# Norm boundaries of a 159-slab transformer kernel: two slabs interleaved by chunk, a third pair of PSUM banks, and the sums of squares on VectorE

## What is computed

```python
for i in range(2):                       # first_block
    h = rms_norm(x, g[i][0])
    h = mlstm_mixer(h, ...) if i == 0 else short_conv_mixer(h, ...)
    x = x + rms_norm(h, g[i][1])         # "post" norm, then the residual
    h = relu(rms_norm(x, g[i][2]) @ w_up[i]) ** 2 @ w_down[i]
    x = x + rms_norm(h, g[i][3])         # "post" norm, then the residual
# second_block
h = rmsnorm(x, mix_norm_g)               # retention and pooling from one projection
x = x + concat([y_ret, y_pool]) @ w_out
x = x + cross_attn(rmsnorm(x, xa_norm_g), rmsnorm(mem, mem_norm_g), ...)
x = x + conv_glu_ffn(rmsnorm(x, ffn_norm_g), ...)
return rmsnorm(x, final_norm_g)
```

## Time and profile before

| | |
|---|---|
| median of 3 runs | 994.25 us (993.46 to 1000.04) |
| the profiled execution | 992.6 us |
| its span, first to last instruction | 990.5 us |
| TensorE busy | 961.8 us (97%) |
| VectorE busy | 648.3 us (65%) |
| ScalarE busy | 537.0 us (54%) |
| GpSimd busy | 144.2 us (15%) |

### The profile page before, as it was taken

One profiled execution on the slowest core, in us unless ns is written; L12 is line 12 of the kernel. 1 busy time (PEld: TensorE's weight loads), 2 busy tenths in 40 slices (PEclk: granted clock), 3 DMA queues, 4 the chain that ended last, 5 costly groups with the idle time before them and its releaser, 6 DMA issues.

```text
span 990.5 us, 20138 instructions
## 1 busy us (share of the span) xinstructions
PE 961.8 (97%) x8062; PEld 950.9 (96%) x8062; DVE 648.3 (65%) x839; ACT 537.0 (54%) x754; POOL 144.2 (15%) x129
## 2 busy tenths in 40 slices
PE   8999989999999899989999999899999999999996
PEld 8999989999999899989999999899999999999995
DVE  6567576665444877587655444894775779999642
ACT  5566656654443555556555444565554557666541
POOL 2121140000010400159000000414120110000001
PEclk9999999999999999999999999999999999999998
DMA  9533636555545355545455553663433545555521
GB/s 337 198 128 111 217 123 207 194 197 191 207 169 202 109 203 191 190 134 207 170 195 188 179 203 113 217 210 130 163 136 127 171 144 197 201 180 177 206 86 43
DMA packets 25844, 172.17 MB, mean 174 GB/s; under 512 B 3252, under 2 KB 3892, under 8 KB 5432
## 3 DMA queue, kind: packets, MB, share of 16 engines
q1 hardware_dynamic: 25784, 171.30, 49.7%
HBM read 170.24 MB, written 1.05 MB: 173 GB/s over the span
## 4 chain that ended last, share of the span: by engine, by line
PE 80%; DVE 7%; issue 1%; POOL 1%; ACT 1%; DVEq 0%; ACTq 0%; POOLq 0%
PE po L403 25%; PE po L404 24%; PE po L405 24%; DVE xnL L1241 3%; DVE wL L1234 2%; PE po L431 1%; PE po L432 1%; PE po L430 1%; POOL rtok L1810 1%; PE pc L732 1%; PE pn L471 1%; PE pn L481 1%; DVE y L1441 0%; PE pn L710 0%; PE pa L710 0%
## 5 line engine op out<-in xcount | busy, mean ns | idle before, releaser
L794 ACT ACTIVATE wH<-raw 128x1024 fp32r<-128x1024 f32 x318 | 335.4, 1059 | 297.9 <-PE po L405 267.5
L1234 DVE TENSOR_TENSOR wL<-raw,wH 128x1024 fp32r<-128x1024 f32 x318 | 387.8, 1244 | 157.0 <-ACT wH L794 156.6
L403 PE MATMUL po<-xnH,wH 128*128 128x256 f32 x1376 | 392.2, 285 | 15.2 <-DVE xnL L1241 12.4
L404 PE MATMUL po<-xnL,wH 128*128 128x256 f32 x1376 | 385.1, 280 | 0.0
L405 PE MATMUL po<-xnH,wL 128*128 128x256 f32 x1376 | 385.1, 280 | 0.0
L403 PEld LDWEIGHTS po<-xnH,wH 128*128 128x128 f32 x1376 | 262.3, 191 | 19.3 <-DVE xnL L1241 10.3
L404 PEld LDWEIGHTS po<-xnL,wH 128*128 128x128 f32 x1376 | 260.4, 189 | 0.2
L405 PEld LDWEIGHTS po<-xnH,wL 128*128 128x128 f32 x1376 | 260.0, 189 | 0.0
L403 PE MATMUL po<-hH,wH 128*128 128x256 f32 x688 | 192.0, 279 | 0.0
L404 PE MATMUL po<-hL,wH 128*128 128x256 f32 x688 | 192.0, 279 | 0.0
L405 PE MATMUL po<-hH,wL 128*128 128x256 f32 x688 | 192.0, 279 | 0.0
(11 more groups left out here) (283 smaller groups left out, 1052.7 us busy)
## 6 DMA issues: line engine op xcount, KB each, us to landing
raw<-in_weights SPq DMA_DIRECT2D x158, 1024.0 KB, 4.8
x<-in_xT SPq DMA_DIRECT2D x4, 256.0 KB, 6.4
raw<-in_weights SPq DMA_DIRECT2D x2, 512.0 KB, 6.3
mem<-in_memT SPq DMA_DIRECT2D x1, 1024.0 KB, 12.7
out<-y SPq DMA_DIRECT2D x4, 256.0 KB, 2.4
decayt<-in_decay SPq DMA_DIRECT2D x1, 512.0 KB, 3.7
poolwt<-in_poolw SPq DMA_DIRECT2D x1, 256.0 KB, 3.7
par<-in_params SPq DMA_DIRECT2D x1, 164.0 KB, 3.4
```

The costliest lines, as they stand in the source:

```text
L403: pe.matmul(psum[:, n, 0:T], wH[w][:, wc], aH[:, ac, :], start=start, stop=False)
L404: pe.matmul(psum[:, n, 0:T], wH[w][:, wc], aL[:, ac, :], start=False, stop=False)
L794: act.activation(wH[b % HL][:, hs], raw[b % RAW][:, hs], ACT.Copy).then_inc(s_hi, 1)
L1234: dve.tensor_tensor(wL[b % HL][:, hs], raw[b % RAW][:, hs], wH[b % HL][:, hs].bitcast(f32), ALU.subtract)\
```

## The change

At each of the four norm boundaries:

- TensorE runs the first two slabs of the next phase (`up0`, `cin`, `up1`, `rq`) together, chunk by chunk (`slab_pair`): chunk k of slab 0, then chunk k of slab 1. It waits for the input per chunk, no longer per pair of chunks.
- `pa` and `pb` become one pair of banks `third`. The key fillers `f0` to `f3` and the third slab (number 2) of each of those phases use it; slab 3 then waits for slab 1's drain. The other groups keep `po[g % 2]`.
- The sums for the new norm are taken in the third slab, after its chunk 0, and the spread after its chunk 3.
- The four adds of squares are on VectorE (four instructions, at the end of its `boundary`), and so are all adds of `y` to `x`; GpSimd keeps only the power there. The first pair of chunks is scaled and added as two single chunks.
- The weight splits, and in `boundary` of ScalarE and VectorE the order of all steps, are laid out anew; VectorE now splits one more half slab before the scaling at boundary 2.

At the two residual boundaries both halves of a split were one after the other; now the next input (`xnH`, `xnL`) of a pair stands between them, the first half ahead of it. The squares and their adds on GpSimd stay there.

```diff
-NORMS = ["pre", "pre", "post", "pre", "post", "pre", "post", "pre", "post", "pre", "pre", "pre", "last"]
+NORMS = ["pre", "pre", "post", "preV", "post", "preV", "post", "preV", "post", "preV", "pre", "pre", "last"]
...
-        pa = ctx.enter_context(nc.psum_tensor("pa", [P, 512], f32))
-        pb = ctx.enter_context(nc.psum_tensor("pb", [P, 512], f32))
+        third = ctx.enter_context(nc.psum_tensor("third", [P, 2, 512], f32))
+        pa, pb = third[:, 0, :], third[:, 1, :]
...
+        in_third = [GROUP0[name] for name in ("f0", "f1", "f2", "f3")]
+        in_third += [GROUP0[name] + 2 for name in ("up0", "cin", "up1", "rq")]
+
+        def place_of(g):
+            return 2 if g in in_third else g % 2
+
         def slot(g):
-            return po[g % 2]
+            return third if g in in_third else po[g % 2]
...
-                if g >= 2:
-                    e, n = DRAIN[g - 2]
+                before = [b for b in range(g) if place_of(b) == place_of(g)]
+                if before:
+                    e, n = DRAIN[before[-1]]
                     pe.wait_ge(s_drain[e], n)
...
+            def slab_pair(name, aH, aL, feed, between={}):
+
+                s, g = SLAB0[name], GROUP0[name]
+                for k in range(8):
+                    pe.wait_ge(s_xn, 8 * feed + k + 1)
+                    for j in range(2):
+                        if k == 0:
+                            slot_free(g + j)
+                        if k % 4 == 0:
+                            weights_ready(s + j, k // 4)
+                        for n in range(2):
+                            mm = products(slot(g + j), n, (s + j) % HL, k, aH, aL, k, k == 0, k == 7)
+                        if k == 3:
+                            mm.then_inc(s_half, 1)
+                        if k == 7:
+                            mm.then_inc(s_slab, 1)
+                    if k in between:
+                        between[k]()
...
+                if NORMS[n] == "preV":
+                    pe.wait_ge(s_sqv, squares_summed(n + 1))
+                else:
+                    pe.wait_ge(s_sqa, squares_added(n + 1))
...
-                for j in range(4):
-                    phase_slab(up, j, xnH, xnL, ready=(s_xn, 4 * feed) if j == 0 else None,
-                               between=norm(n_norm) if j == 1 else {})
+                slab_pair(up, xnH, xnL, feed)
+                for j in range(2, 4):
+                    phase_slab(up, j, xnH, xnL, between=norm(n_norm, 0, 3) if j == 2 else {})
...
-                        slab(i * 4 + (s0 + 4 + j), (s0 + j) % HL, slot(g0 + j), xnH, xnL)
+                        slab(i * 4 + (s0 + 4 + j), (s0 + j) % HL, slot(g0 + 4 + j), xnH, xnL)
...
-            for i in range(12):
-                phase_slab("cin", i, xnH, xnL, ready=(s_xn, 8) if i == 0 else None, between=norm(5) if i == 1 else {})
+            slab_pair("cin", xnH, xnL, 2)
+            for i in range(2, 12):
+                phase_slab("cin", i, xnH, xnL, between=norm(5, 0, 3) if i == 2 else {})
...
-            for i in range(4):
-                phase_slab("rq", i, xnH, xnL, ready=(s_xn, 16) if i == 0 else None, between=norm(9) if i == 1 else {})
+            slab_pair("rq", xnH, xnL, 4)
+            for i in range(2, 4):
+                phase_slab("rq", i, xnH, xnL, between=norm(9, 0, 3) if i == 2 else {})
...
+            def boundary(post, gain, up, value=None):
+
+                def feed_chunk(c):
+                    act.wait_ge(s_xadd, 5 * post + c + 1)
+                    act.activation(xnH[:, c, :], x[:, c, :], ACT.Identity, scale=col(gain, c)).then_inc(s_xnH, 1)
+
+                def feed(p):
+                    feed_hi(p, gain, (s_xadd, 5 * post + p + 2))
+
+                s = SLAB0[up]
                 if value is not None:
-
-                    split(nxt)
+                    split(s, halves=(0,))
+                    feed_chunk(0)
+                    feed_chunk(1)
+                    split(s, halves=(1,))
                     fill_values(value)
-                    nxt += 1
-                for p in range(4):
-
-                    feed_hi(p, gain, (s_xadd if p % 2 else s_xaddV, 2 * post + p // 2 + 1))
-                    if p < 2:
-                        feed_squares(p)
-                split(nxt, halves=(0,))
+                    feed(1)
+                    split(s + 1, halves=(0,))
+                    feed_squares(0)
+                    feed_squares(1)
+                else:
+                    split(s + 1, halves=(0,))
+                    feed_chunk(0)
+                    feed_chunk(1)
+                    feed_squares(0)
+                    split(s + 1, halves=(1,))
+                    feed(1)
+                    feed_squares(1)
+                if value is not None:
+                    split(s + 1, halves=(1,))
+                feed(2)
                 feed_squares(2)
+                feed(3)
                 feed_squares(3)
-                split(nxt, halves=(1,))
...
-                for n in range(4):
+                split(s0 + 2)
+                split(s0 + 3)
+                keep_R(n_norm, Rs[:, :])
+                square(0)
+                square(1)
+                for n in range(2, 4):
                     split(s0 + n + 2)
-                    if n == 0:
-                        keep_R(n_norm, Rs[:, :])
                     square(n)
...
-                split(SLAB0["out2"] + i + 2)
-                feed_pair(i, "gxa", residual("out2")(i))
+                split(SLAB0["out2"] + i + 2, halves=(0,))
+                feed_hi(i, "gxa", residual("out2")(i))
+                split(SLAB0["out2"] + i + 2, halves=(1,))
+                feed_squares(i)
...
-                k.then_inc(s_xn, 1)
+                    k.then_inc(s_xn, 1)
...
             def boundary(n, post, filler, feeds, gain, key):

-                nxt = SLAB0[filler] + 1
-                two = nxt == SLAB0[f"f{key}"]
-                split(nxt, halves=(0,))
+                first = SLAB0[filler] + 1
+                two = first == SLAB0[f"f{key}"]
+                split(first, halves=(0,))
                 mean_square(n)
-                split(nxt, halves=(1,))
-                if two:
-                    split(nxt + 1, halves=(0,))
-
+                split(first, halves=(1,))
+                split(first + 1, halves=(0,))
                 dve.wait_ge(s_R, n + 1)
...
-                    dve.tensor_tensor(xs, xs, ys, ALU.add).then_inc(s_xaddV, 1)
-
-                scale(0)
-                add(0)
+                    dve.tensor_tensor(xs, xs, ys, ALU.add).then_inc(s_xadd, 1)
+
+                link(dve.tensor_tensor(y[:, 0, :], y[:, 0, :], pn[:, 128:128 + T], ALU.mult))
+                dve.tensor_tensor(x[:, 0, :], x[:, 0, :], y[:, 0, :], ALU.add).then_inc(s_xadd, 1)
+                dve.tensor_tensor(y[:, 1, :], y[:, 1, :], pn[:, 128:128 + T], ALU.mult).then_inc(s_t, 1)
+                dve.wait_ge(s_t, 4 * post + 1)
+                dve.tensor_tensor(x[:, 1, :], x[:, 1, :], y[:, 1, :], ALU.add).then_inc(s_xadd, 1)
+                feed_pair(feeds, 0, gain)
                 scale(1)
+                add(1)
+                split(first + 1, halves=(1,))
                 scale(2)
-                feed_pair(feeds, 0, gain)
+                if two:
+                    split(first + 2, halves=(0,))
+                feed_pair(feeds, 1, gain)
+                add(2)
                 scale(3)
-                add(2)
+                feed_pair(feeds, 2, gain)
                 if two:
-                    split(nxt + 1, halves=(1,))
-                for p in (1, 2, 3):
-                    feed_pair(feeds, p, gain)
+                    split(first + 2, halves=(1,))
+                add(3)
+                feed_pair(feeds, 3, gain)
+                dve.wait_ge(s_sq, 4 * (n + 1) + 2)
+                dve.tensor_tensor(sq[0], sq[0], sq[1], ALU.add)
+                dve.wait_ge(s_sq, 4 * (n + 1) + 4)
+                link(dve.tensor_tensor(sq[2], sq[2], sq[3], ALU.add))
+                link(dve.tensor_tensor(sq[0], sq[0], sq[2], ALU.add))
+                dve.tensor_tensor(sq[0][:, 0, :], sq[0][:, 0, :], sq[0][:, 1, :], ALU.add).then_inc(s_sqv, 1)
                 fill_keys(key)
-                split(nxt + 2 if two else nxt + 1)
...
+            def norm_and_split(n, s, both=False):
+
+                if both:
+                    split(s, halves=(0,))
                 mean_square(n)
-                split(s, halves=(0,))
-                split(s, halves=(1,))
+                split(s, halves=(1,) if both else (0, 1))
+                if both:
+                    split(s + 1)
                 dve.wait_ge(s_Rs, kept_before(n)[0] + 1)
...
+                norm_and_split(n_norm, s0 + 2, both=True)
+                for n in range(2):
                     relu(n)
-                    if n:
-                        split(s0 + n + 2)
+                for n in range(2):
+                    hidden(n)
+                for n in range(2, 4):
```

(8 more changed lines are left out.)

71 lines of the change are left out of this document (34 added, 37 removed).

## The result

The changed kernel takes **967.95 us** (median of 4, 967.62 to 970.08) where the kernel before took 997.14 beside it (4 executions, 993.46 to 1000.42): ratio 0.972, 95% interval 0.968 to 0.976. The forecast was 982 with a range of 973 to 991. The direction held, the size didn't: the first result lies 5 us under the range, and the second median is inside it only because four of its six executions are some 6 us above the rest.

What follows compares the result with a forecast made beforehand. TensorE, busy 97% of the span, was taken as the bound. Losses of 17.5 us less new waits of 2.35 and 2.4 gave 12.7: 992.6 to 979.9, plus 1.65 to the median and 0.4 for thin covers, 982 us; range 973 to 991.

Steps and rivals of the forecast that it cites:

- the first rival: A block of some 30 slabs may flip its pace, 6.3 us either way: 976 (chance 0.12) or 988 (0.14).
- The waits: TensorE's losses at the four norm and two residual boundaries: 17.5 us, less new waits of 2.35 and 2.4, gain 12.7.
- Boundary 1: Into `up0`: step-by-step list of solo lengths leaves no wait in the slab pair, gain 3.3 us.
- the third rival: VectorE instructions stay slow because ScalarE, not GpSimd, doubled them: 28 us more, 1010 us, chance 0.06.
- Boundary 2: Into `cin`, with one filler: new loss of 2.35 us for the old 5.7, gain 3.35 us.
- Boundary 3: Into `up1`: same list as at boundary 1, gain 3.2 us.
- Boundary 4: Into `rq`: pair's 3.5 us wait goes, new 2.4 us wait at `rq.3` for the drain of `rq.1`; gain 1.1.
- Residual boundaries: At `wq.0` and `fup.0`: last pair's `xnL` follow the residual add directly, gains of 1.0 and 0.8 us.
- The second rival: Third slab's weights late at each norm boundary, about 1 us each, `rq.3` and `cin.3` more: 987 us, chance 0.18.
- The fourth: Slab pair waits for weights, `up0.1`'s first half coming after 136.2: 1 us per boundary, counted inside the 0.18 late-slab case.

Runs made afterwards that it cites:

- the second median: The changed kernel unaltered, compared again with the kernel before on another chip: 974.96 us (6 executions), 0.980 of before.
- banks_only: The kernel before with the third pair of banks alone, nothing else changed: 985.51 us, 0.991 of before.
- residual_undone: The changed kernel with the two residual boundaries put back as they were before: 975.59 us, 0.981 of before.
- banks_and_early_norm: The kernel before with the third pair of banks, and the norm's sums and spread one chunk earlier in `wq.1` and `fup.1`: 980.12 us, 0.993 of before.
- sums_on_gpsimd: The changed kernel with the sums of squares at the four norm boundaries back on GpSimd: 972.78 us.
- not_interleaved: The changed kernel with the first two slabs of each phase one after the other instead of by chunk: 976.1 us, 0.989 of before.

## Why the prediction was wrong, step by step

**The step that failed is the pace: the sum put it at nothing, and the first rival at one block.** The prediction read the two paces rightly, and named the mechanism ("a changed start of the blocks may flip either"), but priced it as a coin with two sides, one block of 6.3 us at 0.12 and 0.14. Measured was 12.15 us, two blocks, both to the faster side; 979.9 less that is 967.8, and the profiled execution took 968.0. Three things were missed. First, that a fast `up1` was to be expected: the change gives slab 2 of `up1` a bank that is free, and with it the stall at its start goes, as in all nine traces without a stall there, each with `up1` at 5.44 a slab; I wrote of covers under 1 us at the third slab and never looked at what TensorE did after the 0.20 us there in before. `banks_only` gives that part alone, 8 us in the median. Second, that there is a third block, `fup` and `fdown`, 31 slabs at 5.65 in before. In after it was at 5.44; `residual_undone` and `banks_and_early_norm` show that the reordered residual isn't needed for it, and its stall at `fup.2` is still there. Why its pace came out fast behind the spread in `fup.1`, and whether the change had a part in that or luck alone, stays open: `sums_on_gpsimd` had it slow. Third, that the profiled execution of before, near the median (994.25), had two slow blocks of three, so that there was more to win than to lose.

**The waits were right in sum**, in part by luck: the forecast had 12.7 us and the stretches give 12.4, but `wq.0` fell 0.9 short and boundaries 3 and 4 and `fup.0` came out 0.8 over, some of it pace. The groups of times say the same without any stretch: if the four fastest executions of before (median 980.97) and the four of after at 967.6 to 968.6 (median 967.95) have all blocks at the faster pace, what is left between them is 13.0.

- **Boundary 1**: 3.3 us forecast, 3.4 measured. The list held almost to the tenth. Its end on VectorE in after:

```profile
135.15 0.88 DVE L1303 SCALAR_TENSOR_TENSOR xnL<-x,par,xnH 128x256 fp32r<-128x256 f32 x2
...
140.40 0.88 DVE L1303 SCALAR_TENSOR_TENSOR xnL<-x,par,xnH 128x256 fp32r<-128x256 f32 x2 [0.58 <-ACT xnH L842]
...
143.59 0.68 DVE L1325 TENSOR_TENSOR memk<-third,Rm 128x512 f32<-128x512 f32 x1
144.19 1.22 DVE L1296 TENSOR_TENSOR wL<-raw,wH 128x1024 fp32r<-128x1024 f32 x1
```

  Low parts of pair 1 at 136.0 (forecast 136.4), of pair 3 at 141.3 (141.7), the key drain at 144.3 (144.8), the half of `up0.2` at 145.4 (146.0), with `f0` ending 0.42 us earlier than in before. Each `xnL` costs 0.44 us beside an idle GpSimd, for 0.99 in the earlier trace rows, and the half split 1.22 for 2.32, and GpSimd had no instruction from 127.5 to 147.9: the third rival (VectorE stays slow) is out. The Trainium skill ("SBUF — State Buffer", "Who interferes with whom") says that a VectorE instruction with two SBUF inputs contends with a GpSimd one that reads SBUF; these numbers agree.
- **Boundary 2**: 3.35 forecast, 3.0 measured. TensorE's starts stand 1.14 us apart at chunk 0, 1.39 at chunk 2 and 0.57 at the third slab; less one matmul, 1.03 (forecast 0.7), 1.28 (1.25) and 0.46 (0.4). The clock stayed at its upper level, where the trace of before had a stretch at the lower one.
- **Boundary 3**: 3.2 forecast; 3.70 measured, of which 0.3 is pace (two slabs at 5.44 for 5.65).
- **Boundary 4**: 1.1 forecast, 1.3 measured, as a new wait of 2.2 us for 2.4 at `rq.3`. The list was right: first drain to second drain in after is

```profile
628.22 0.68 DVE L1325 TENSOR_TENSOR rq<-po,Rs 128x512 f32<-128x512 f32 x1
...
631.58 0.68 DVE L1325 TENSOR_TENSOR rq<-po,Rs 128x512 f32<-128x512 f32 x1
```

  3.36 us. What I left out is that the stall can drop the clock: 1.4 to 1.5 us more in all five other traces that have this wait.
- **Residual boundaries**: forecast 1.0 and 0.8, measured 0.1 and 0.8. For `wq.0` the step "Now they follow the residual add directly and end near 724.5" (they are the last pair's two `xnL`) failed in its start: the residual add itself came late. The timeline of after, the first residual add on VectorE, then VectorE, ScalarE and GpSimd around the last pair:

```profile
686.93 3.49 DVE L1296 TENSOR_TENSOR wL<-raw,wH 128x1024 fp32r<-128x1024 f32 x3
690.34 0.68 DVE L1719 TENSOR_TENSOR x<-x,po 128x512 f32<-128x512 f32 x1
...
701.55 0.67 DVE L1719 TENSOR_TENSOR x<-x,po 128x512 f32<-128x512 f32 x1
...
704.02 0.61 ACT L845 ACTIVATE squares<-x 128x512 f32<-128x512 f32 x1
...
704.54 1.04 ACT L828 ACTIVATE wH<-raw 128x1024 fp32r<-128x1024 f32 x1
704.71 1.81 POOL L1879 TENSOR_TENSOR squares<-squares 128x512 f32<-128x512 f32 x1 [4.17 <-ACT squares L845]
...
705.62 1.99 DVE L1296 TENSOR_TENSOR wL<-raw,wH 128x1024 fp32r<-128x1024 f32 x1 [0.24 <-ACT wH L828]
707.53 0.68 DVE L1719 TENSOR_TENSOR x<-x,po 128x512 f32<-128x512 f32 x1
```

  The last add starts 2.7 us behind the end of `out2.3` (704.87), and that has two parts. The first add was already 1.8 us late (690.34, `out2.0` ended at 688.55), behind three half splits in a row. And the three turns from add to add take 5.21, 6.00 and 5.98 us, where TensorE's slabs come every 5.44: in the two long ones the half split waits for ScalarE's squares and half, and then takes 1.99 us beside GpSimd's add. Behind `wo` the turns are as long (5.65, 6.00, 5.99), but the first add comes 0.2 us behind `wo.0`, the last 0.9 behind `wo.3`, and the wait was gone, as forecast; so it was in the two traces with `wo` at 5.44 a slab (`sums_on_gpsimd`, `not_interleaved`). I had counted the last turn of the loop, and neither its start nor its period.

The second rival (late third slabs) cost 0.3 us in the view of waits, all at boundary 2, not 5. The fourth (the pair waits for weights) didn't come: the pair of boundary 1 took 11.31 us with TensorE busy throughout.

## What to carry to other kernels

Before counting waits, compare the distance of matmuls from start to start in stretches without any wait, over several executions: where the same code shows two paces, look at the first stall or batch of small matmuls ahead of each stretch, at the pace on both sides of it, and price a change of it over the whole stretch behind it. A spare bank that takes away a stall of 0.1 us may be worth more than an order of work that takes away three. For a loop of steps over several engines, work out when its first turn starts and its period against TensorE's, not only its last turn; and when a stall is put on TensorE knowingly, take into account that it can cost the clock as well.

## What the runs showed of the hardware

- Matmuls of 256 columns, each with its own weights, follow one another at 113.3 or 117.8 ns (152.32 and 158.29 us for the same 28 slabs of 48) at a granted clock of 1.00. The pace held for 30 slabs once taken. Its changes fell on a stall, on the norm's small matmuls, or on the step from a value filler (weights as the moving operand) to a key filler, where no start is over 0.125 us from the last (after, 129.4: 113 ns, then 118; `banks_only`, 129.7: 118, then 113). A stall doesn't always change it: none of twelve at `fup.2` did. What chooses is open: the restart put into `up0` went to the slower pace in both traces, the one in `up1` stayed at the faster in all three, and the stall of 0.2 us in before went both ways in `up0`.
- Over 71 executions of one kernel the times spread from 980.5 to 1001.5 us, in four groups that stand about one block's difference in pace apart. With the stall at `rq.3` gone, four versions spread over 1.4 to 2.9 us each in 23 executions (the one of 5430.48 us left out), where the changed kernel spread over 9.7 in ten; why that stall should reach the pace of a later block wasn't tested.
- After a stall of 2.2 us at `rq.3` TensorE ran some fifteen matmuls of 0.213 us at the lower clock level in five traces, and none in a sixth. Behind the stall of 2.6 us at boundary 2 of the kernel before and its two versions with the new banks it did so in three traces of four.
